# Spreading the expert gates eight tokens at a time, in one buffer and four banks, with part of the one-hot products on ScalarE

## The reference

```
q = (xf @ wq).reshape(T, PEER_HEADS, 2, PEER_KEY_DIM)
s = jnp.einsum('thcd,ckd->thck', q, subkeys)
sv, si = lax.top_k(s, PEER_TOPK)
cand = (sv[:, :, 0, :, None] + sv[:, :, 1, None, :]).reshape(T, PEER_HEADS, PEER_TOPK * PEER_TOPK)
cv, ci = lax.top_k(cand, PEER_TOPK)
ea = jnp.take_along_axis(si[:, :, 0], ci // PEER_TOPK, axis=-1)
eb = jnp.take_along_axis(si[:, :, 1], ci % PEER_TOPK, axis=-1)
experts = (ea * PEER_KEYS + eb).reshape(T, PEER_HEADS * PEER_TOPK)
gate = jax.nn.softmax(cv, axis=-1)
act = jax.nn.gelu(jnp.einsum('cd,ced->ce', xc, u_tab[ec]))
y = jnp.einsum('ce,ced->cd', act * gc, v_tab[ec])
```

## Time and profile before

| | |
|---|---|
| median of 3 runs | 3087.29 us (3086.4 to 3103.18) |
| profiled execution, its own time | 3087.28 us |
| its span | 3085.5 us |
| mean granted clock of TensorE | 0.954 |
| PE, DVE, ACT, POOL busy | 2828.8, 2225.6, 1604.9, 82.9 us |
| the 128x1024 splits on DVE, all units | 994.2 us |
| matmuls of the spread, 512 | 85.3 us |
| squares for the one-hot rows, 512 | 162.6 us |

### The profile page before, as it was taken

The page is one execution under the profiler, slowest core; times in us unless marked ns, Lnnn a source line. Parts: engine busy times, 40 slices in busy tenths (PEclk is TensorE's granted clock), DMA queues, the critical chain, the costliest instruction groups (busy, mean ns, idle before and its releaser), DMA issues.

```text
span 3085.5 us, 46430 instructions
## 1 busy us (share of the span) xinstructions
PE 2828.8 (92%) x17816; PEld 2520.9 (82%) x17816; DVE 2225.6 (72%) x3602; ACT 1604.9 (52%) x2733; POOL 82.9 (3%) x141
## 2 busy tenths in 40 slices
PE   6888799899799997999999999989798999999997
PEld 3675599786699876989999888878698999988886
DVE  2753566676555555899898878874579998977887
ACT  2333244334344353467888554545445778855453
POOL 1000000010000200000000000020000000000000
PEclk8889899899899988999999999998799999999999
DMA  7323567576355623556656877763255656587775
GB/s 254 111 62 116 191 226 252 181 230 206 116 178 182 208 77 102 182 186 204 193 190 205 265 241 242 241 207 117 70 178 180 202 189 198 190 264 242 243 241 161
DMA packets 211610, 580.28 MB, mean 188 GB/s; under 512 B 24032, under 2 KB 87808, under 8 KB 210112
## 3 DMA queue, kind: packets, MB, share of 16 engines
q1 hardware_dynamic: 162704, 495.20, 50.4%
q0 software_dynamic: 12976, 49.60, 4.9%
q10 hardware_dynamic: 35712, 32.52, 3.1%
HBM read 541.57 MB, written 35.65 MB: 187 GB/s over the span
## 4 chain that ended last, share of the span: by engine, by line
PE 73%; DVE 17%; ACT 6%; issue 2%; DMA 1%; ACTq 0%; POOL 0%; DVEq 0%; POOLq 0%
PE psum L692 72%; DVE wr L1895 4%; DVE gmem L1895 4%; DVE oh_r L1895 3%; ACT gmem L1352 2%; DVE gmem L1898 2%; ACT wr L1352 2%; ACT crf L1352 1%; PE psum L735 1%; DVE xmem L1898 1%; ACT L1352 1%; DVE gmem L2663 1%; DVE gmem L2076 0%; ACT xmem L1352 0%; ACTq L1838 0%
## 5 line engine op out<-in xcount | busy, mean ns | idle before, releaser
L1895 DVE TENSOR_TENSOR wr<-raw,wr 128x1024 fp32r<-128x1024 f32 (+1 forms) x814 | 994.2, 1223 | 494.5 <-ACT wr L1352 492.6
L692 PE MATMUL psum<-xr,wr 128*128 128x256 f32 x10464 | 1314.4, 286 | 31.0 <-DVE wr L1895 14.8
L692 PEld LDWEIGHTS psum<-xr,wr 128*128 128x128 f32 x10464 | 1289.3, 195 | 44.9 <-DVE xr L1895 14.5
L1352 ACT ACTIVATE wr<-raw 128x1024 fp32r<-128x1024 f32 (+1 forms) x814 | 853.8, 1049 | 320.7 <-PE psum L692 271.5
L692 PE MATMUL psum<-wr,cr 128*128 128x512 f32 x3072 | 696.8, 389 | 3.0 <-DVE cr L1895 3.0
L692 PEld LDWEIGHTS psum<-wr,cr 128*128 128x128 f32 x3072 | 576.6, 188 | 122.7 <-ACT cr L1352 3.3
L1352 ACT ACTIVATE gmem<-psum 128x512 f32<-128x512 f32 (+2 forms) x307 | 162.0, 540 | 276.2 <-PE psum L692 242.4
L1352 ACT ACTIVATE cr<-xmem 128x256 fp32r<-128x256 f32 x256 | 107.2, 419 | 341.9 <-PE psum L692 339.9
L692 PE MATMUL psum<-wr,xr 128*128 128x512 f32 (+1 forms) x960 | 242.3, 410 | 21.0 <-DVE xr L1895 11.0
L692 PEld LDWEIGHTS psum<-wr,xr 128*128 128x128 f32 x960 | 184.5, 200 | 68.3 <-issue 15.0
L692 PE MATMUL psum<-gmem 128*128 128x128 f32 (+8 forms) x1352 | 196.1, 299 | 17.2 <-DVE gmem L1895 13.6
(11 more groups left out here) (143 smaller groups left out, 1652.8 us busy)
## 6 DMA issues: line engine op xcount, KB each, us to landing
raw<-in_uv SPq DMA_DIRECT2D x512, 512.0 KB, 4.8
raw<-in_ffn_in SPq DMA_DIRECT2D x88, 512.0 KB, 4.1
gs<-xmem ACTq DMA_DIRECT2D x248, 128.0 KB, 3.7
xmem<-gs SPq DMA_DIRECT2D x248, 128.0 KB, 4.5
raw<-in_ada_w SPq DMA_DIRECT2D x48, 512.0 KB, 4.0
gmem<-in_ada_w POOLq DMA_DIRECT2D x48, 512.0 KB, 4.7
raw<-in_ffn_out SPq DMA_DIRECT2D x44, 512.0 KB, 3.5
raw<-in_ret_a SPq DMA_DIRECT2D x32, 512.0 KB, 4.3
```

The costliest lines, as they stand in the source:

```text
L692: ins = pe.matmul(o, a, b, start=first and i == 0, stop=final and i == len(pairs) - 1, skip_group_check=skip)
L1352: return act.activation(o, a, func, **k)
L1895: return dve.tensor_tensor(o, a, b, op)
```

## The change

A group now has eight tokens, 16 groups for each half of the tokens (17 rounds). There is one buffer `oh` (the second buffer's 1024 words and the first's 1024 are joined), one `oha` and one set of banks, 4 to 7. In round i, first step: ACT copies out group i-1, then makes eight squares and one relu for group i; DVE adds group i-1, then makes the comparison and the high product of group i. Second step: ACT makes the low product of tokens 4 to 7 by four copies with a scale, DVE that of tokens 0 to 3, and PE multiplies group i. The step costs are changed to 2.3 and 2.2.

```diff
-    oh = [v.rearrange("p (j s n) -> p j s n", j=4, s=2) for v in (ohr0, ohr1)]
+    oh = ohr.rearrange("p (j s n) -> p j s n", j=8, s=2)
-    spread_ = [2.2, 0.75] * 34
+    spread_ = [2.3, 2.2] * 17
 # PE
-            for i in range(34):
-                yield
-                if 0 < i < 33:
-                    g = (i - 1) % 2
-                    claim(4 + 2 * g, 5 + 2 * g)
-                    pe.wait_ge(*Z.dve["oh", l, a, i - 1])
-                    pe.wait_ge(*Z.act["oh", l, a, i - 1])
-                    for j in range(4):
+            for i in range(17):
+                yield
+                if i < 16:
+                    claim(4, 5, 6, 7)
+                    pe.wait_ge(*Z.dve["oh", l, a, i])
+                    pe.wait_ge(*Z.act["oh", l, a, i])
+                    for j in range(8):
...
 # ACT
+            for i in range(17):
+                if i > 0:
+                    t8 = 128 * a + 8 * (i - 1)
+                    act.wait_ge(*Z.pe[l, a, i - 1])
+                    f(gmat[:, t8:t8 + 8, :].rearrange("p (b j) e -> p b j e", b=4),
+                      bank(4, 4).rearrange("p b (j s e) -> p b j s e", j=2, s=2)[:, :, :, 1, :],
+                      AF.Copy).then_inc(*Z.act.up(("g", l, a, i - 1)))
...
+                if i < 16:
+                    for j in range(8):
+                        f(ohaf[:, j, :], iota, AF.Square, bias=keep[:, 1, tk:tk + 1]).then_inc(*Z.act.up())
+                    act.wait_ge(*Z.act.now)
+                    f(oha, ohaf, AF.Relu, scale=-1.0, bias=1.0).then_inc(*Z.act.up())
+                yield
+                if i < 16:
+                    act.wait_ge(*Z.dve["hi", l, a, i])
+                    for j in range(4, 8):
+                        f(oh[:, j, 1, :], oh[:, j, 1, :].bitcast(F32), AF.Copy,
+                          scale=keep[:, 3, tk:tk + 1]).then_inc(*Z.act.up(("oh", l, a, i) if j == 7 else None))
+                yield
 # DVE
+            for i in range(17):
+                if i > 0:
+                    dve.wait_ge(*Z.act["g", l, a, i - 1])
+                    tt(d, d, bank(4, 4)..., ALU.add).then_inc(*Z.dve.up(("g", l, a, i - 1)))
...
+                if i < 16:
+                    tt(lo, bc(iota.unsqueeze(1), [P, 8, 128]), key, ALU.is_equal).then_inc(*Z.dve.up())
+                    own(Z)
+                    tt(hi, lo.bitcast(F32), g_hi, ALU.mult).then_inc(*Z.dve.up(("hi", l, a, i)))
+                yield
+                if i < 16:
+                    own(Z)
+                    tt(lo[:, 0:4], lo[:, 0:4].bitcast(F32), g_lo, ALU.mult).then_inc(*Z.dve.up(("oh", l, a, i)))
+                yield
```

More of the change, by code:

```diff
@@ L223, in program @@
     o_x = at[0]
-    xmem, ohr1 = place("xmem", 2048), place("oh_r1", 1024, F32R, o_x + 4096)
+    xmem, ohm, ohr = place("xmem", 2048), place("oh", 1024), place("oh_r", 2048, F32R, o_x + 4096)
     wr = place("wr", NSPLIT * 2048, F32R).rearrange("p (i s n) -> p i s n", i=NSPLIT, s=2)
@@ L229, in program @@
     keepm, keepr = place("keep", 1024), place("keep_r", 1024, F32R, o_keep)
-    o_oh = at[0]
-    ohm, ohr0 = place("oh", 1024), place("oh_r0", 1024, F32R, o_oh)
     rawm = place("raw", NRAW * UNIT)
@@ L466, in program @@
     cu3 = ci[:, 0:128].bitcast(U32).rearrange("p (h k) -> p h k", h=8)
-    oh = [v.rearrange("p (j s n) -> p j s n", j=4, s=2) for v in (ohr0, ohr1)]
-    oha = cr.rearrange("p (i j n) -> p i j n", i=2, j=4)
-    ohaf = crf.rearrange("p (i j n) -> p i j n", i=2, j=4)
+    oh = ohr.rearrange("p (j s n) -> p j s n", j=8, s=2)
+    oha = cr.rearrange("p (j n) -> p j n", j=8)
+    ohaf = crf.rearrange("p (j n) -> p j n", j=8)
     gel = [xmem[:, i * 256:(i + 1) * 256] for i in range(8)]
@@ L501, in program @@
     pick, rest = [1.5, 1.0] * 8, [1.4] + [1.8, 1.0] * 4 + [0.8] + [1.2] * 12 + [0.7, 0.9, 0.5]
-    spread_ = [2.2, 0.75] * 34
-    both = [v for i in range(68) for v in spread_[i:i + 1] + (pick + rest)[i:i + 1]]
+    spread_ = [2.3, 2.2] * 17
+    both = [v for i in range(len(pick + rest)) for v in spread_[i:i + 1] + (pick + rest)[i:i + 1]]
     costs = pick[-4:] + rest + both + spread_
@@ L1293, in spread @@
             pe.wait_ge(*Q.dve["keep", l, a])
-            for i in range(34):
+            for i in range(17):
                 yield
-                if 0 < i < 33:
-                    g = (i - 1) % 2
-                    claim(4 + 2 * g, 5 + 2 * g)
-                    pe.wait_ge(*Z.dve["oh", l, a, i - 1])
-                    pe.wait_ge(*Z.act["oh", l, a, i - 1])
-                    for j in range(4):
[L1303 to L1306, removed]
+                if i < 16:
[3 more added lines that the diff above has]
+                    for j in range(8):
+                        ins = mm(bank(4 + j // 2)[:, 256 * (j % 2):256 * (j % 2) + 256],
+                                 [(oha[:, j, :], oh[:, j].rearrange("p s n -> p (s n)"))])
+                    ins.then_inc(*Z.pe.up((l, a, i)))
+                    for b in range(4):
+                        drained[4 + b] = Z.dve["g", l, a, i]
                 yield
@@ L1807, in spread @@
             act.wait_ge(*Q.dve["keep", l, a])
[L1808 to L1817, removed]
-                    act.wait_ge(*Z.act.now)
[L1819 to L1827, removed]
-                yield
+            for i in range(17):
[5 more added lines that the diff above has]
+                      AF.Copy).then_inc(*Z.act.up(("g", l, a, i - 1)))
+                elif a:
+                    act.wait_ge(*Z.pe[l, 0, 15])
+                if i < 16:
+                    for j in range(8):
+                        tk = 128 * a + 8 * i + j
+                        f(ohaf[:, j, :], iota, AF.Square, bias=keep[:, 1, tk:tk + 1]).then_inc(*Z.act.up())
+                    act.wait_ge(*Z.act.now)
+                    f(oha, ohaf, AF.Relu, scale=-1.0, bias=1.0).then_inc(*Z.act.up())
+                yield
+                if i < 16:
+                    act.wait_ge(*Z.dve["hi", l, a, i])
+                    for j in range(4, 8):
+                        tk = 128 * a + 8 * i + j
+                        f(oh[:, j, 1, :], oh[:, j, 1, :].bitcast(F32), AF.Copy,
+                          scale=keep[:, 3, tk:tk + 1]).then_inc(*Z.act.up(("oh", l, a, i) if j == 7 else None))
@@ L2688, in spread @@
             dve.wait_ge(*Q.dve["keep", l, a])
[L2689 to L2702, removed]
+            for i in range(17):
+                if i > 0:
+                    t8 = 128 * a + 8 * (i - 1)
+                    dve.wait_ge(*Z.act["g", l, a, i - 1])
+                    d = gmat[:, t8:t8 + 8, :].rearrange("p (b j) e -> p b j e", b=4)
+                    tt(d, d, bank(4, 4).rearrange("p b (j s e) -> p b j s e", j=2, s=2)[:, :, :, 0, :],
+                       ALU.add).then_inc(*Z.dve.up(("g", l, a, i - 1)))
+                elif a:
+                    dve.wait_ge(*Z.pe[l, 0, 15])
+                else:
+                    dve.wait_ge(xs_out[l], 16)
+                tk = slice(128 * a + 8 * i, 128 * a + 8 * i + 8)
+                hi, lo = oh[:, :, 0, :], oh[:, :, 1, :]
+                if i < 16:
+                    key, g_hi = (bc(v[:, tk].unsqueeze(2), [P, 8, 128]) for v in (keep[:, 0, :], gate_hi.bitcast(F32)))
+                    tt(lo, bc(iota.unsqueeze(1), [P, 8, 128]), key, ALU.is_equal).then_inc(*Z.dve.up())
@@ L2703, in spread @@
                     own(Z)
-                    tt(hi, lo.bitcast(F32), g_hi, ALU.mult).then_inc(*Z.dve.up())
+                    tt(hi, lo.bitcast(F32), g_hi, ALU.mult).then_inc(*Z.dve.up(("hi", l, a, i)))
+                yield
+                if i < 16:
+                    g_lo = bc(keep[:, 3, tk][:, 0:4].unsqueeze(2), [P, 4, 128])
                     own(Z)
-                    tt(lo, lo.bitcast(F32), g_lo, ALU.mult).then_inc(*Z.dve.up(("oh", l, a, i)))
-                yield
[L2708 to L2714, removed]
+                    tt(lo[:, 0:4], lo[:, 0:4].bitcast(F32), g_lo, ALU.mult).then_inc(*Z.dve.up(("oh", l, a, i)))
@@ L2787, in reload @@
             if e == 4:
-                sp.wait_ge(*Z.dve["g", l, 1, 31])
+                sp.wait_ge(*Z.dve["g", l, 1, 15])
             if e >= 8:
@@ L2893, in pool_program @@
             load(i16, const("iota16"), sub_in[l])
-            pool.wait_ge(*Z.dve["g", l, 1, 31])
+            pool.wait_ge(*Z.dve["g", l, 1, 15])
             pool.wait_ge(*W.pe[base_v[l] - 1])
```

## The result

The changed kernel takes 3481.48 us in the median (3480.83 to 3488.26, 4 runs); the kernel before, run beside it again, 3094.06 us. The ratio is 1.1249, with a 95% interval of 1.1208 to 1.1289: 12.5% slower. The forecast was 3471 us and 12.4%. The runs of the kernel before lie in two clusters, 3086 to 3091 us and 3097 to 3103 us, with mean granted clocks of 0.952 to 0.954 and 0.947 to 0.949 where the clock is on record, so differences of half a per cent or less say little here.

The account below looks back on a forecast made before the run. TensorE was taken to bound the first half of each layer's expert phase. The sum was 3087 + 304 (stalls) + 96 (slower clock) - 16 (earlier idle time replaced) = 3471 us, 12.4% slower, range 3340 to 3560 us.

Parts of the forecast that it names:

- The bound: First half of each layer's expert phase: TensorE limits it, with 22.7 us idle in both layers together.
- The coupling and the stall in the late part: Late groups, 16 a layer: ScalarE's work starts only after TensorE's unit, so TensorE stalls 4.9 us per group.
- The stall in the early part: Early groups, 16 a layer, sharing steps with the router: TensorE stalls 4.6 us before each group's matmuls.
- The clock: TensorE behind each of 64 stalls: 3 us at half speed, 1.5 us lost each, 96 us in all.
- Rival (a): TensorE in the expert stretches: granted clock holds at 1.00 through the stalls, 3375 us; chance 20%.
- rival (b): TensorE behind each stall: clock stays low for all of the path, 246 us, total 3621 us; chance 10%.
- (c): Second step of each group: only its own work is late, stalls of 1.6 us, total 3173 us; chance 7%.
- (d): Expert stretches: products ready when TensorE arrives, lighter VectorE removes 20 us of waits, 3067 us; chance 5%.
- these two terms: Busy time over 64 groups: VectorE's falls by 75 us, ScalarE's rises by 79 us.

Follow-up runs that it names:

- one edit: Changed kernel with TensorE's eight matmuls of a group moved one step later, into the first step of the next round: 3169.58 us, ratio 1.0249.
- the kernel with groups of four: Kernel before the change, with TensorE multiplying group i in the second step of round i, not of round i+1: 3604.95 us, ratio 1.1662.

## Why the prediction was right

The mechanism was right: the coupling, the engine that waits, the place of the loss and the fall of the clock. Of the two sizes the idle time came out a little smaller than forecast and the clock's cost larger, and part of the closeness of the sum is luck.

**The bound.** TensorE had 22.7 us to give in the windows of the earlier trace rows. VectorE is busy 58 us less, and the span still grew by the whole of the new idle and busy time of TensorE, 393.4 us.

**The coupling and the stall in the late part.** 4.9 us was worked out, 4.93 measured in the timeline above. The steps of the sum are there one by one: 0.28 from gelu to copy, 2.47 for eight squares, 0.96 for the relu, the split, the next gelu, and VectorE's half product last, from 1762.13. Of the 16 late groups of a layer 15 stall for 4.93 to 5.02 us; the first one stalls for 1.73 us, so the mean is 4.7.

**The stall in the early part.** 4.6 us was taken for each. The timeline of TensorE shows 4.62, and 5.53 where the second step comes one unit sooner:

```profile
1389.67 2.05 PE L691 MATMUL psum<-oh_r,cr 128*128 128x256 f32 x8 [4.62 <-DVE oh_r L1897]
1391.52 10.42 PE L691 MATMUL psum<-xr,wr 128*128 128x256 f32 x72
1407.46 2.05 PE L691 MATMUL psum<-oh_r,cr 128*128 128x256 f32 x8 [5.53 <-DVE oh_r L1897]
```

They are two of many. The waits of TensorE for the rows over the whole program (us, times, longest) are

```profile
PE psum L691 <- DVE oh_r L1897: 280.9, 58, 6.4
...
PE psum L691 <- ACT oh_r L1351: 10.4, 6, 1.7
```

The timeline shows the six as the stalls of 1.73 us; two of them are the late ones named above. Over the 32 early groups the stalls run from 1.73 to 6.43 us, with a mean of 4.4, so the one value of 4.6 came near the average and did not hold group by group. Together 304 - 16 = 288 us of idle time were forecast, and it rose by 278.5.

**The clock.** 96 us was taken, as 3 us at half speed behind each of 64 stalls, and the busy time of TensorE rose by 115 us in the windows. The fall is as forecast, its size is not. The 58 stalls of 3.79 us and more were all followed by half speed, the six of 1.73 us were not. Behind a late stall half speed lasted longer than 3 us: in the 4 us from 1763.06 the granted clock is 0.50, and a cycle lost 2.1 us and not 1.5. So the term was 19 us too small and that of the stalls 10 too large, and the sum of 384 us stands beside 393.4 measured. Rival (a), a clock that holds, falls with the granted clock of 0.83; rival (b), half speed for all of the path, asks for 246 us and was about twice too large. That the length of a short stop does not settle what the clock does is visible before the change too: behind the 2.01 us stop of the earlier trace rows it fell, and behind another of 2.01 us, at 1484.58 in the same trace, it stayed at 1.00 for 6 us.

**The other rivals.** (c), only the second step is late, asks for stalls of 1.6 us; that fits only the six of 1.73 us, and 58 of 64 are longer. (d) falls with the idle time of 291 us in front of the spread matmuls.

**What else was off.** The busy time of VectorE fell by 58 us and not by 75, that of ScalarE rose by 57 and not by 79. I had multiplied counts by mean durations, but consecutive operations overlap in the records, as the 0.60 us between two operations of 0.68 us in the earlier trace rows shows, and the page counts an overlap within an engine's busy time once. The sum of the time did not use these two terms.

## What to carry to other kernels

When an engine's queue asks for data in the same step in which the others make it, and one of those must first wait for that engine, each group costs the length of their work, less what the waiting engine still has to do meanwhile. Before larger groups or a shift of load are judged by busy time, write down for the waiting engine when it asks and when its supplier can start. Here that distance was worth 312 us from one edit, the shift of products to ScalarE 29. And where a stall can't be avoided, count the slower clock behind it as part of its price.

## What the runs showed that I had not expected

When I made the prediction I had not thought that more matmuls could make the kernel faster: 64 groups of 36 took it from 3481.48 to 3390.13 us, and 64 groups of 24, which leave some 2 us of each stall idle, to 3424.46. Half speed behind a stall was also more regular than expected: in the changed kernel eight spread matmuls took 2.04 or 2.05 us behind all 58 stalls of 3.79 to 6.43 us, and 1.19 behind the six of 1.73 us. In the kernel with groups of four, behind stalls of the same 3.55 us, four matmuls took 0.71 us at one group and 1.20 us at others, so the length of the stop alone doesn't decide whether the clock is already down at the return. It fell all the same: of the 50 stalls of 3.55 us, 14 were followed by matmuls at full speed, and the mean granted clock of the next 4 us was 0.69 or less behind every one of them (0.68 behind 1717.03). What decides the moment, these runs don't show.
